# Hyena convolutions in a diffusion block: all spectral products on VectorE, skip terms on ScalarE, another order of the inverse and output products

## The reference

```python
def _fft_conv(u, kern, skip):
    n, L = kern.shape[0], u.shape[1]
    y = jnp.fft.irfft(jnp.fft.rfft(u, n=n, axis=1) * jnp.fft.rfft(kern, axis=0)[None], n=n, axis=1)[:, :L]
    return y + u * skip

def _hyena_seq(h, w_in, b_in, conv_w, conv_b, kern, skip, w_out, b_out):
    ...
    v, x1, x2 = jnp.split(u.astype(F32), 3, -1)
    z = x1 * _fft_conv(v, kern[:, 0], skip[0])
    y = x2 * _fft_conv(z, kern[:, 1], skip[1])
    return y.astype(h.dtype) @ w_out + b_out
```

## Time and profile before

| | |
|---|---|
| median of 3 runs | 2057.25 us (2056.12 to 2063.15) |
| profiled execution | 2058.01 us, its span 2056.2 us (1.8 us lie around the span) |
| `hyena_convolutions` in the profile | 1432.3 to 1542.2 us from the span's start |
| busy over the whole span | PE 88%, DVE 38%, ACT 26%, POOL 9% |
| granted TensorE clock, mean | 0.945 of full |

### The profile page before, as it was taken

How to read it: one execution, slowest core, us unless ns; L and a number is a source line. 1 busy time by engine, 2 the same in 40 slices (tenths; PEclk the granted TensorE clock), 3 DMA queues, 4 the chain that set the end, 5 groups by cost and what they waited for, 6 DMA issues and landing times. The chain is left out here.

```text
span 2056.2 us, 34476 instructions
## 1 busy us (share of the span) xinstructions
PE 1810.3 (88%) x13981; PEld 969.5 (47%) x13981; DVE 778.6 (38%) x1841; ACT 538.2 (26%) x990; POOL 175.5 (9%) x121
## 2 busy tenths in 40 slices
PE   3868798888887887999999997899888999999996
PEld 1435555545555535444444443568546344444442
DVE  4766675676676534301100101723753411100101
ACT  2244544543543402111111112131202111111111
POOL 0512102102102000000000000000510000000000
PEclk8879999999999897999999999998997999999999
DMA  9013322322323557999999997212344999999993
GB/s 294 0 56 88 98 84 77 104 88 83 103 90 103 176 192 300 422 428 428 428 428 428 428 413 233 82 41 83 142 167 171 425 428 428 428 428 428 428 411 139
DMA packets 105566, 504.04 MB, mean 245 GB/s; under 512 B 16032, under 2 KB 60816, under 8 KB 79648
## 3 DMA queue, kind: packets, MB, share of 16 engines
q1 hardware_dynamic: 103488, 501.88, 61.6%
q10 hardware_dynamic: 1952, 0.39, 0.1%
HBM read 501.13 MB, written 1.09 MB: 244 GB/s over the span
## 5 line engine op out<-in xcount | busy, mean ns | idle before, releaser
L2005 DVE TENSOR_TENSOR arena<-banks,arena 128x512 f32<-128x512 f32 x32 | 22.1, 692 | 661.4 <-PE banks L1820 661.4
L1820 PE MATMUL banks<-arena 128*64 128x512 f32 x1024 | 226.4, 594 | 11.0 <-DMA arena<-in_moe_w_up 11.0
L1842 PE MATMUL banks<-arena 128*64 128x512 f32 x1024 | 226.8, 595 | 3.3 <-ACT arena L1936 3.3
L1811 PE MATMUL banks<-arena 128*64 128x512 f32 x1024 | 225.3, 592 | 3.3 <-DVE arena L1928 3.3
L800 PE MATMUL banks<-arena 128*128 128x512 f32 (+1 forms) x384 | 159.1, 552 | 0.8 <-ACT arena L1109 0.8
L1820 PEld LDWEIGHTS banks<-arena 128*64 128x64 f32 x1024 | 82.5, 137 | 153.2 <-issue 153.2
L1811 PEld LDWEIGHTS banks<-arena 128*64 128x64 f32 x1024 | 74.3, 137 | 147.8 <-issue 144.2
L1842 PEld LDWEIGHTS banks<-arena 128*64 128x64 f32 x1024 | 70.7, 137 | 154.5 <-issue 150.7
L1930 ACT ACTIVATE arena<-banks,arena 128x128 f32<-128x128 f32 x128 | 48.2, 457 | 340.6 <-PE banks L1800 340.6
L1800 PEld LDWEIGHTS banks<-arena 128*128 128x128 f32 x1024 | 121.0, 198 | 28.1 <-issue 24.3
L1800 PE MATMUL banks<-arena 128*128 128x128 f32 x1024 | 127.1, 284 | 3.5 <-DVE arena L2000 3.5
(11 more groups left out here) (386 smaller groups left out, 2591.0 us busy)
## 6 DMA issues: line engine op xcount, KB each, us to landing
arena<-in_moe_w_gate SPq DMA_DIRECT2D x64, 2048.0 KB, 14.9
arena<-in_moe_w_up SPq DMA_DIRECT2D x64, 2048.0 KB, 17.1
arena<-in_moe_w_down SPq DMA_DIRECT2D x64, 2048.0 KB, 13.3
arena<-in_ada_w SPq DMA_DIRECT2D x128, 192.0 KB, 2.9
arena<-in_ada_w SPq DMA_DIRECT2D x64, 256.0 KB, 3.6
arena<-in_rw_wrkv SPq DMA_DIRECT2D x24, 512.0 KB, 5.1
arena<-in_hy_w_in SPq DMA_DIRECT2D x6, 2048.0 KB, 8.7
arena<-in_ada_w SPq DMA_DIRECT2D x8, 1024.0 KB, 16.8
```

The costliest lines, as they stand in the source:

```text
L1811: mm = pe.matmul(G[j * CAP:(j + 1) * CAP, :], xT[:, t, j * CAP:(j + 1) * CAP], wg[par][j][:, t], start=(t == 0), stop=(t == KT - 1))
L1820: mm = pe.matmul(U[j * CAP:(j + 1) * CAP, :], xT[:, t, j * CAP:(j + 1) * CAP], wu[j][:, t], start=(t == 0), stop=(t == KT - 1))
L1842: mm = pe.matmul(bank[j * CAP:(j + 1) * CAP, :], hT[:, t, j * CAP:(j + 1) * CAP], wd[j][:, t, half * 512:(half + 1) * 512], start=(t == 0) ...
L2005: dve.tensor_tensor(h, U[:, :], sg, ALU.mult).then_inc(h_ready, 1)
```

## The change

Four edits, all in `hyena_convolutions`. The imaginary part of the spectral product moves from POOL to DVE, behind the real part of the same half; POOL has no work left in this block. The inverse takes, for each half of the channels, first the real part of all four tiles (waiting for `real_ready` alone) and then the imaginary part (waiting for `imag_ready`). The skip term moves from DVE to ACT, which does all eight tiles of a convolution after its last `vhat` copy, in place, with a new semaphore `skip_ready`. The output product runs m outermost for the first four tiles only; for the last four the bank is outermost, so banks end one after the other.

```diff
@@ tensor
-                for m in range(CH):
-                    if m % 4 == 0:
-                        pe.wait_ge(real_ready, od * 2 + m // 4 + 1)
-                        pe.wait_ge(imag_ready, od * 2 + m // 4 + 1)
-                    k = 0
+                for half in range(2):
                     for part in range(2):
-                        for ft in range(2):
-                            mm = pe.matmul(s.psum[m // 2][:, m % 2 * L:(m % 2 + 1) * L], prod[:, part, ft, m * P:(m + 1) * P], inv[part][:, ft],
-                                           start=(k == 0), stop=(k == 3))
-                            k += 1
-                    if m % 2:
-                        mm.then_inc(y_done, 1)
+                        pe.wait_ge((real_ready, imag_ready)[part], od * 2 + half + 1)
+                        for m in range(4 * half, 4 * half + 4):
+                            for ft in range(2):
+                                mm = pe.matmul(s.psum[m // 2][:, m % 2 * L:(m % 2 + 1) * L], prod[:, part, ft, m * P:(m + 1) * P], inv[part][:, ft],
+                                               start=(m % 2 == 0 and part == 0 and ft == 0), stop=(m % 2 == 1 and part == 1 and ft == 1))
+                            if part == 1 and m % 2:
+                                mm.then_inc(y_done, 1)
+
+            def out_product(m, k):
+                i, h = divmod(k, 2)
+                return pe.matmul(s.psum[4 + k][:, :], u[:, m, i * P:(i + 1) * P], w_out[:, m, h * 512:(h + 1) * 512],
+                                 start=(m == 0), stop=(m == CH - 1))
+
             pe.wait_ge(vhat_ready, 16)
-            for m in range(CH):
+            for m in range(CH // 2):
                 pe.wait_ge(y_ready, 9 + m)
...
+                for k in range(4):
+                    out_product(m, k)
+            pe.wait_ge(wout_in[1], 16)
+            for k in range(4):
+                for m in range(CH // 2, CH):
+                    if k == 0:
+                        pe.wait_ge(y_ready, 9 + m)
+                    mm = out_product(m, k)
+                mm.then_inc(o_done, 1)
@@ scalar
+                for m in range(CH):
+                    act.activation(u[:, m], u[:, m], ACT.Copy, scale=skip[:, od * CH + m:od * CH + m + 1]).then_inc(skip_ready, 1)
@@ gpsimd
-                    pool.wait_ge(vhat_ready, (od * 2 + half) * 4 + 4)
-                    pool.tensor_tensor(prod[:, 1, :, c], vhat[:, 0, :, c], khat[:, od, 1, :, c], ALU.mult)
-                    pool.tensor_tensor(half_b, vhat[:, 1, :, c], khat[:, od, 0, :, c], ALU.mult)
-                    pool.drain()
-                    pool.tensor_tensor(prod[:, 1, :, c], prod[:, 1, :, c], half_b, ALU.add).then_inc(imag_ready, 1)
-                    pool.drain()
@@ vector
                     dve.tensor_tensor(prod[:, 0, :, c], prod[:, 0, :, c], half_a, ALU.subtract).then_inc(real_ready, 1)
+                    dve.tensor_tensor(prod[:, 1, :, c], vhat[:, 0, :, c], khat[:, od, 1, :, c], ALU.mult)
+                    dve.tensor_tensor(half_b, vhat[:, 1, :, c], khat[:, od, 0, :, c], ALU.mult)
+                    dve.drain()
+                    dve.tensor_tensor(prod[:, 1, :, c], prod[:, 1, :, c], half_b, ALU.add).then_inc(imag_ready, 1)
                     dve.drain()

                 for m in range(CH):
                     dve.wait_ge(y_done, od * 4 + m // 2 + 1)
-                    dve.tensor_scalar(u[:, m], u[:, m], skip[:, od * CH + m:od * CH + m + 1], None, ALU.mult)
-                    dve.drain()
+                    dve.wait_ge(skip_ready, od * CH + m + 1)
```

More of the change, by code:

```diff
@@ L2566, in hyena_layer @@
         ("vT_done", "vt_ready", "dft_done", "vhat_ready", "real_ready", "imag_ready", "y_done", "y_ready"))
-    o_done = S("o_done")
+    o_done, skip_ready = S("o_done"), S("skip_ready")
     with nc.Block(name="hyena_convolutions", no_gpsimd_drain=True) as block:
@@ L2616, in _ @@
+            def out_product(m, k):
+                i, h = divmod(k, 2)
+                return pe.matmul(s.psum[4 + k][:, :], u[:, m, i * P:(i + 1) * P], w_out[:, m, h * 512:(h + 1) * 512],
+                                 start=(m == 0), stop=(m == CH - 1))
             pe.wait_ge(vhat_ready, 16)
-            for m in range(CH):
+            for m in range(CH // 2):
                 pe.wait_ge(y_ready, 9 + m)
[L2619 to L2626, removed]
+                if m == 0:
+                    pe.wait_ge(wout_in[0], 16)
+                for k in range(4):
+                    out_product(m, k)
```

## The result

The changed kernel takes 2042.2 us (median of 4 runs, 2041.38 to 2045.33) against 2059.74 us for the kernel before in the same comparison (4 runs): ratio 0.9921, 95% interval 0.99 to 0.9941. So it is faster by 0.6 to 1.0%. In a later comparison the same kernel had 2042.42 us and a ratio of 0.9916 (0.9891 to 0.9941). The profiled execution took 2041.48 us with a span of 2039.7, 16.5 us less than before. The forecast was 2043.9 in a range of 2040.0 to 2047.0, from a gain of 13.3.

The account below looks back on a forecast made before the run. PE was taken to bound the block, with no slack behind it to absorb gains. 9.46 us (inverses) plus 3.82 (tail) made 13.3; 2058.01 less that is 2044.7, with the median 0.76 lower 2043.9, range 2040.0 to 2047.0.

Parts of the forecast that it names:

- likeliest case: Whole kernel: the summed gain of 13.3 us arrives, giving 2042.5 to 2045.5 us; chance 72%.
- the step on the stream of loads: Expert layer: gate loads start after the router, so what the block gives up makes everything after it earlier.
- Spectral products: hyena_convolutions: both parts on DVE without POOL, 1.14 us from start to start, 7.22 us per half.
- the reading of the earlier trace as turns: Spectral products: DVE and POOL take turns, so long durations of DVE's operations hold one POOL turn.
- Inverse: PE's inverse in each convolution: gaps before and inside it close, 4.73 us gained each, 9.46 in sum.
- the 1.69 us lost before: First convolution's inverse: first batch returns from 8.83 to 7.14 us at full clock; a 6% rival denied this.
- the sum would be about the same: Inverse: old order with both parts on DVE would gain about the same 9.46 us.
- Skip: Epilogue: moving skip terms from DVE to ACT is worth 0, as the work hides either way.
- the bound of 3.8: ACT's eight skip operations of 128x256, at 0.47 us each, take at most 3.8 us.
- Tail: Behind the output product: only three DVE operations remain, 2.34 us instead of 6.16, a gain of 3.82 us.
- a full clock in all the logits: Router rival: shorter pause keeps the clock up, 48 instructions run 5.3 us faster, 2038.6 us; chance 14%.
- part of them: Router rival's partial case: only part of the 48 logit instructions at full clock, 2041 us or so.

Follow-up runs that it names:

- pool_adds: Changed kernel plus three GpSimd additions of 128x1024 per half on columns nothing else uses; block 108.78 us against 96.03, span 2051.8.
- pool_fills: Changed kernel plus GpSimd fills of 128x1024, two in place of each addition on unused columns, reading no SBUF; block 96.30 us, span 2039.5.
- busy_again: Changed kernel plus, in both layers' routers, four 128x512 TensorE products during top-k and two before the gather; 2034.2 us, ratio 0.9886 to the kernel before.

## Why the prediction was right

**The number.** The time lay in the range, 1.7 us under the forecast, but that nearness is partly luck. The gain was 16.5 us between the profiles and 17.5 between the medians of the comparison, not 13.3; the median of the kernel before was 2059.74 there, 2.5 above the 2057.25 that the forecast started from, and hid part of the difference. What was missing is 0.9 in the block and 2.5 in the router. The likeliest case by itself, 2042.5 to 2045.5, just missed the 2042.2.

**Where the gain lands.** Nothing absorbed it: 14.23 us in the block arrive at the end with 0.2 lost behind the third pair's load, as the step on the stream of loads said.

**Spectral products.** The step that decided was the reading of the earlier trace rows as turns. It is shown by pool_adds and pool_fills, which give and take the turns without any shared data, and by 7.24 us for a half against the 7.22 forecast.

**Inverse.** Forecast 4.73 us per convolution, measured 5.20. The mechanism was right and the term too small by 0.47: I counted two batches of 7.14 us, 14.28, per inverse, but 64 instructions without a break take 13.98; and I let the inverse start at the recorded end of the forward row (1446.06 + 7.13 = 1453.19), where it starts 0.16 earlier, at 1453.03. The clock stayed at full, so the 1.69 us lost before came back, as assumed. Moving the products alone is worth 7.53 us, and the edit of the order 2.75 on top of it; the prediction's sentence that without the new order "the sum would be about the same" was wrong by those 2.75, since it looked at half 0 and forgot half 1, for which its own times give a wait (imaginary part at 1460.9, PE free at 1460.15).

**Skip.** 0 forecast, 0.01 measured. ACT's eight took 3.29 us, under the bound of 3.8.

**Tail.** 3.82 forecast, 3.90 and 3.82 measured.

**Router.** I took 0 and gave 14% to a full clock in all the logits, worth 5.3 us. Measured are 2.5 us, the first 16 of 48 logit instructions at full clock and about half of the next 16: the rival's own case of "part of them", which it put at 2041 or so. The cause that I had named for it, the shorter pause, does not decide it, and what does stays open. So a term of the sum that stood at 0 was 2.5 us, and the range held because it had room for that. With it the terms add up: 14.2 for the block and 2.5 for the router are 16.7, and the two ratios of the changed kernel give 16 and 17.

## What to carry to other kernels

Two engines that split elementwise work may be slower than one, as 10.0 us against 7.24 show here: if the durations beside each other are about the sum of both prices, compute the price from an operation whose neighbour was idle, and put the work on the faster engine. Let an accumulation over banks end bank by bank when another engine must finish each bank, and order a consumer's work by which input comes first. When whole times spread by more than the change, read the length of the stage, not the span.

## What the runs showed of the hardware that was not expected

TensorE's clock in the changed kernel, from windows of PE alone (us, PE busy, PEclk, DMA share, GB/s):

```profile
1532.00:1534.00 2.00, 1.64 (x15) 1.00 1.00 426
1534.00:1536.00 2.00, 2.00 (x16) 0.77 1.00 426
1536.00:1538.00 2.00, 2.00 (x12) 0.50 1.00 426
```

The logits, products with 36 columns, are back to back, and the clock still falls from 1.00 to 0.50 under them, while it came back under the eight instructions of 512 columns of busy_again (0.50 from 1542 to 1544, 1.00 from 1546 to 1548). Transfers were at a full share in these windows, but they are not needed for a fall: under the 1-column products L2384, also back to back, the clock went from 1.00 (1421 to 1424) to 0.50 (1427 to 1430) at a DMA share of 0.03 and less. An engine that the profile calls fully busy can lose its clock. The Trainium skill (TensorE: Matmul & The Clock Gate, the section on why this matters) warns of long idle gaps between bursts of matmuls; here avoiding them was not enough, and a pause of 1.76 us cost the gather its clock in one layer and not in the other of the same run.
